# Attention by pairs of heads: scores as rounded-operand products on half the array rows, value products issued alternately into two column halves

## The reference

```python
# first network, mixers A, B and C, each with 8 heads of 64
s = einsum(q, k_all)                       # 256 latent + 256 context keys
# A: no mask;  B: + bias of the neighbourhood;  C: band mask, a sink logit per head
p = softmax(s);  y = einsum(p, v_all)
yc = einsum(softmax(einsum(qc, kc)), vc)   # context queries, first layer only
ux = concatenate([ya, yb, yc_]) * silu(px[9]);  x = x + gate * (ux @ w_out)
# second network, each layer: 8 heads over compressed, selected and window keys,
# gated and summed, and 8 heads of causal attention of its own
o = gate0 * o_cmp + gate1 * o_sel + gate2 * o_win
```

## Time and profile before

| | us |
|---|---|
| median of 3 runs | 2254.88 (2253.24 to 2255.66) |
| span of the profiled execution | 2251.3 |
| PE busy | 2108.9 (94%) |
| PE weight loads busy | 1909.6 (85%) |
| DVE busy | 1317.9 (59%) |
| ACT busy | 1136.5 (50%) |
| POOL busy | 40.8 (2%) |

### The profile page before, as it was taken

The page is one execution under the profiler, slowest core; times in us unless marked ns, Lnnn a source line. Parts: engine busy times, 40 slices in busy tenths (PEclk is TensorE's granted clock), DMA queues, the critical chain, the costliest instruction groups (busy, mean ns, idle before and its releaser), DMA issues.

```text
span 2251.3 us, 40100 instructions
## 1 busy us (share of the span) xinstructions
PE 2108.9 (94%) x15086; PEld 1909.6 (85%) x15086; DVE 1317.9 (59%) x2238; ACT 1136.5 (50%) x1994; POOL 40.8 (2%) x49
## 2 busy tenths in 40 slices
PE   6799999999799899799999999999899998989997
PEld 5767976966569776699999889999899998889997
DVE  5755238447662466566556767664665546766654
ACT  5455236256552546466354555553565445555653
POOL 2000002000000010000000000000000000000000
PEclk9899989999999999899989999999999989999999
DMA  8221223121122322155544224555455443234553
GB/s 294 110 81 60 87 93 112 64 87 57 57 75 76 126 71 75 42 183 186 182 156 150 77 94 169 178 179 185 151 180 176 173 146 114 103 121 169 186 187 131
DMA packets 41625, 289.35 MB, mean 129 GB/s; under 512 B 4656, under 2 KB 5696, under 8 KB 7440
## 3 DMA queue, kind: packets, MB, share of 16 engines
q1 hardware_dynamic: 39344, 279.99, 34.8%
q0 software_dynamic: 2144, 7.48, 1.0%
HBM read 286.40 MB, written 1.05 MB: 128 GB/s over the span
## 4 chain that ended last, share of the span: by engine, by line
PE 86%; DVE 5%; ACT 5%; issue 2%; DMA 2%; DVEq 0%; ACTq 0%; SPq 0%
PE bank L1503 23%; PE bank L1505 22%; PE bank L1504 22%; PE bank L1592 6%; PE bank L1635 5%; PE bank L1620 3%; DMA raw_panels<-weights 2%; ACT panels_hi L604 1%; DVE panels_lo L1000 1%; PE bank L1579 1%; PE bank L1571 1%; ACT kT_padded L710 1%; PE bank L1545 1%; DVE softmax_stats L1086 1%; PE bank L1555 1%
## 5 line engine op out<-in xcount | busy, mean ns | idle before, releaser
L604 ACT ACTIVATE panels_hi<-raw_panels 128x1024 fp32r<-128x1024 f32 x532 | 547.5, 1052 | 800.1 <-PE bank L1505 774.4
L1000 DVE TENSOR_TENSOR panels_lo<-raw_panels,panels_hi 128x1024 fp32r<-128x1024 f32 x532 | 641.5, 1225 | 510.1 <-ACT panels_hi L604 508.9
L1503 PE MATMUL bank<-acts_hi,panels_hi 128*128 128x256 f32 (+2 forms) x3072 | 899.1, 293 | 15.2 <-DVE acts_lo L1137 6.6
L1505 PE MATMUL bank<-acts_hi,panels_lo 128*128 128x256 f32 (+2 forms) x3072 | 891.5, 290 | 0.0
L1504 PE MATMUL bank<-acts_lo,panels_hi 128*128 128x256 f32 (+2 forms) x3072 | 891.3, 290 | 0.0
L1503 PEld LDWEIGHTS bank<-acts_hi,panels_hi 128*128 128x128 f32 x3072 | 592.2, 193 | 26.7 <-DVE xT L1273 5.5
L1504 PEld LDWEIGHTS bank<-acts_lo,panels_hi 128*128 128x128 f32 x3072 | 592.3, 193 | 8.1
L1505 PEld LDWEIGHTS bank<-acts_hi,panels_lo 128*128 128x128 f32 x3072 | 592.2, 193 | 7.5
L1503 PE MATMUL bank<-panels_hi,acts_hi 128*128 128x256 f32 (+1 forms) x1056 | 309.1, 293 | 19.3 <-DVE acts_lo L1032 19.3
L1504 PE MATMUL bank<-panels_lo,acts_hi 128*128 128x256 f32 (+1 forms) x1056 | 305.6, 289 | 0.0
L1505 PE MATMUL bank<-panels_hi,acts_lo 128*128 128x256 f32 (+1 forms) x1056 | 305.3, 289 | 0.0
(11 more groups left out here) (166 smaller groups left out, 1644.5 us busy)
## 6 DMA issues: line engine op xcount, KB each, us to landing
raw_panels<-weights SPq DMA_DIRECT2D x266, 1024.0 KB, 4.8
near_bias<-rpb POOLq DMA_DIRECT2D x16, 256.0 KB, 3.0
xT<-xin POOLq DMA_DIRECT2D x4, 512.0 KB, 5.9
out<-xT SPq DMA_DIRECT2D x1, 1024.0 KB, 4.5
consts_sb<-consts POOLq DMA_DIRECT2D x1, 789.5 KB, 8.2
small_layers<-small POOLq DMA_DIRECT2D x1, 184.0 KB, 8.1
small_sb<-small POOLq DMA_DIRECT2D x1, 168.0 KB, 8.1
smallg_sb<-smallg POOLq DMA_DIRECT2D x1, 16.0 KB, 5.4
```

The lines of the kernel that those rows point to most:

```text
L604: act.activation(slot_hi(n, a, b), raw[:, (n % 2) * PAN + a:(n % 2) * PAN + b], ACT.Copy).then_inc(hi_ready, 1)
L1000: dve.tensor_tensor(slot_lo(n, a, b), raw[:, (n % 2) * PAN + a:(n % 2) * PAN + b], slot_hi(n, a, b).bitcast(F32), ALU.subtract).then_inc(l ...
L1503: pe.matmul(dst, whi_, xhi_, start=start, stop=False, skip_group_check=True)
L1505: return pe.matmul(dst, wlo_, xhi_, start=False, stop=stop, skip_group_check=True)
```

## The change

The loop runs over **steps** instead of units. A step is one pair of heads with 128 queries (for context queries and the causal heads: one pair of heads with all 256 queries), so two units at once.

- Queries and keys are kept in two parts, rounded and low (`qT_split`, `kT_split`), without padding. A score is three products of rounded operands on the 64 rows of its head; the products of the two heads alternate.
- The value products work on 128 queries at a time for a latent pair, and the two heads, which write to the two halves of the partitions, alternate product by product.
- Four score banks instead of three; the turned probabilities of a step fill two banks and are copied by one ACT instruction over both; one output bank instead of two. The steps behind are i-2 (turnings and copy), i-3 (values), i-4 (gating, rounding), i-5 (low part).
- In the turn stage ACT makes the rounded part in one copy (`turns_hi`), DVE subtracts for the low part (`turns_lo`), and only then is the bank free. The compressed keys are split in the same way, and their scores are three products of rounded operands each.
- A woven panel is rounded and split whole in one iteration, the one after its slot. The slots are 1, 4, 7, 10 and 0, 1, 3, 4, 6, 7, 9, 10.
- A bias tile holds the two heads of a step instead of the two query blocks of a head. The zero padding of the keys, and PE's waits for it, are gone.

```diff
-    qT = sb("qT", 2048)
-    kP = sb("kT_padded", 4096)
+    qT = sb("qT_split", 2 * 2048, F32R)
+    kT = sb("kT_split", 2 * 2048, F32R)
...
+    def q_split(p, e, t0):
+        return [q_of(half, p, t0)[e] for half in range(2)]
+
+    def k_split(i, e, per, t0, t1):
+        return [kT[e * HD:(e + 1) * HD, half * 2048 + i * per + t0:half * 2048 + i * per + t1] for half in range(2)]
...
@@ attention_plan, latent steps of the first network
+            for p in range(NPAIR):
+                idx = p // 2 if gqa else p
                 for qt in range(TT):
+                    units, adds = [], []
+                    for e in range(2):
...
+                        units.append(Unit([(q_split(p, e, qt * P), k_split(idx, e, 512, 0, 512), 0, 512)],
+                                          [(0, 512, h if mixer == "C" else None, None)], masks,
+                                          [(b * P, b * P) for b in range(4)]))
+                    for b in range(4):
+                        for e in range(2):
+                            vcol = (p // 2 if gqa else 2 * p + e) * HD
+                            adds.append((e, val(b, vcol), e * 512 + b * P, P, qt * P, b == 0))
+                    steps.append(Step(units, [(0, 512)], adds, len(pairs), qt == 0, qt == 1))
...
@@ ACT, in the loop
+                j = i - 2
+                if 0 <= j < len(steps):
+                    g = g0 + j
+                    act.wait_ge(probT, now(probT, g + 1))
+                    if g >= 2:
+                        act.wait_ge(pv, now(pv, g - 1))
+                    for c, n in steps[j].copies:
+                        o = act.activation(by_head(probsT(g), c, n), by_head(prob_banks, c, n), ACT.Copy)
+                    o.then_inc(probT_out, 1)
...
@@ DVE
+        def turns_lo(b, k, hi, lo, scale=1.0):
+
+            dve.wait_ge(turn_hi, now(turn_hi, k + 1))
+            dve.scalar_tensor_tensor(lo, tile4(turn_bank(b)[:, :], lo.shape[1]), scale, hi.bitcast(F32), ALU.mult,
+                                     ALU.subtract).then_inc(turn_out, 1)
...
@@ PE, in the loop
-                    for k, (keys, c, w) in enumerate(un.keys):
-                        o = pe.matmul(score_bank(u)[:, c:c + w], un.q, keys, start=True, stop=True, skip_group_check=True)
-                    o.then_inc(scores, 1)
+                    for k in range(len(units[0].parts)):
+                        for a, b in ((0, 0), (0, 1), (1, 0)):
+                            for e in range(2):
+                                q, keys, c, w = units[e].parts[k]
+                                o = pe.matmul(score_bank(2 * g + e)[:, c:c + w], q[a], keys[b], start=a + b == 0, stop=a == 1,
+                                              skip_group_check=True)
...
+                    for k, (e, v, c, n, q0, start) in enumerate(step.adds):
+                        o = pe.matmul(out_bank[e * HD:(e + 1) * HD, q0:q0 + n], v, probsT(g)[:, c:c + n],
+                                      start=start, stop=k >= len(step.adds) - 2, skip_group_check=True)
```

More of the change, by code:

```diff
@@ L395, in program, with q_of @@
         blocks: list
-        qt: int
-        group: int
     @dataclass
-    class Group:
+    class Step:
+        units: list
+        copies: list
         adds: list
         pair: int
+        first: bool
         last: bool
         cmp: bool = False
-        head: object = None
+    def q_of(half, p, t0):
+        q = qT[:, half * 2048:(half + 1) * 2048].rearrange("p (a t) -> p a t", a=4)
+        return [q[e * HD:(e + 1) * HD, p, t0:t0 + P] for e in range(2)]
+    def q_split(p, e, t0):
+        return [q_of(half, p, t0)[e] for half in range(2)]
+    def k_split(i, e, per, t0, t1):
+        return [kT[e * HD:(e + 1) * HD, half * 2048 + i * per + t0:half * 2048 + i * per + t1] for half in range(2)]
     def attention_plan(blk, mixer, with_ctx):
-        units, groups, pairs = [], [], []
-        qv = qT[:, :].rearrange("p (a t) -> p a t", a=4)
+        steps, pairs = [], []
         def val(tt, col):
@@ L444, in attention_plan @@
-                    adds = []
+                    idx = p // 2 if gqa else p
+                    units, adds = [], []
                     for e in range(2):
                         h = 2 * p + e
-                        vcol = (h // 4 if gqa else h) * HD
-                        adds += [(e, val(2 + b, vcol), 2 * e + b, 0, b == 0) for b in range(2)]
-                    groups.append(Group(adds, len(pairs), True))
-                    pairs.append((p, 1))
-            return units, groups, pairs
@@ L459, in attention_plan @@
+                    for b in range(2):
+                        for e in range(2):
+                            vcol = (p // 2 if gqa else 2 * p + e) * HD
+                            adds.append((e, val(2 + b, vcol), e * 512 + b * T, T, 0, b == 0))
+                    steps.append(Step(units, [(0, 512)], adds, len(pairs), True, True))
+                    pairs.append((p, 1))
+            return steps, pairs
+        for p in range(NPAIR):
+            g = p // 2
             for qt in range(TT):
@@ new lines, in attention_plan @@
+                for k in range(2):
+                    for b in range(qt + 1):
+                        for e in range(2):
+                            v = VS2 + b * 256 + k * P + g * HD
+                            adds.append((e, tok[:, v:v + HD], e * 512 + (2 * k + b) * P, P, qt * P, False))
+                copies = [(k * T, P) for k in range(2)] if qt == 0 else [(0, 512)]
+                steps.append(Step(units, copies, adds, len(pairs), qt == 0, qt == 1, cmp=qt == 0))
+            pairs.append((p, 0))
@@ L487, in attention_plan @@
             pairs.append((p, 1))
-        return units, groups, pairs
-    def last_unit_of(units, g):
-        return max(i for i, u in enumerate(units) if u.group == g)
+        return steps, pairs
     def merge_gate_place(r):
@@ L655, in attention @@
         def attention(blk, mixer, with_ctx, st):
-            units, groups, pairs = attention_plan(blk, mixer, with_ctx)
-            u0, g0, p0 = st.at["units"], st.at["groups"], st.at["pairs"]
-            for i in range(len(units) + 7):
+            steps, pairs = attention_plan(blk, mixer, with_ctx)
+            g0, p0 = st.at["groups"], st.at["pairs"]
+            for i in range(len(steps) + 4):
                 for r, slot in enumerate(ADA_SLOTS if st.panels and blk == 1 else ()):
@@ L700, in attention @@
-                j = i - 6
-                if 0 <= j < len(units) and last_unit_of(units, units[j].group) == j and groups[units[j].group].last:
-                    pr = groups[units[j].group].pair
+                j = i - 2
[7 more added lines that the diff above has]
+                    o.then_inc(probT_out, 1)
@@ L1281, in _ @@
                 gate(m)
+                b = ONE["turn" + m, l].at["turns"]
+                for tt in range(nt):
+                    turns_lo(b, b, q_turned(0, tt), q_turned(1, tt), HD ** -0.5)
+                    b += 1
+                for tt in range(4 if m == "B" else 2):
+                    turns_lo(b, b, k_turned(0, m, tt), k_turned(1, m, tt))
+                    b += 1
                 attention(1, m, wctx, ONE["attn" + m, l])
@@ L1409, in _ @@
             split_panel(m0 + 3)
+            b = TWO["turn_nsa"].at["turns"]
+            for tt in range(TT):
+                turns_lo(b + tt, b + tt - 2, q_turned(0, tt), q_turned(1, tt), HD ** -0.5)
             dve.wait_ge(cm_act, now(cm_act, 2))
@@ new lines, in attention @@
+                j = i - 3
+                if 0 <= j < len(steps):
+                    g, step = g0 + j, steps[j]
+                    pe.wait_ge(probT_out, now(probT_out, g + 1))
+                    if step.first and p0 + step.pair >= 1:
+                        pe.wait_ge(omul, now(omul, p0 + step.pair))
+                    if step.cmp:
+                        pr = pairs[step.pair][0]
+                        pe.matmul(out_bank[:, 0:T], vblk[:, pr * P:(pr + 1) * P], pcT, start=True, stop=False,
```

433 lines of the change are left out of this document (199 added, 234 removed).

## The result

The changed kernel is slower, by half a per cent: 2263.6 us (median of 14 runs, 2257.8 to 2269.0) against 2253.3 for the kernel before beside it (14 runs, 2248.8 to 2256.0), ratio 1.0047, 95% interval 1.0037 to 1.0056. The forecast was 2220, faster.

The account below looks back on a forecast made before the run. PE was taken as the bound, with 86% of the chain. Attention stages -48.6, waits +5, turn stages +8.5 gave -35; 2251.3 - 35 + 3.6 = 2220 us, range 2208 to 2234, chance 0.62.

Parts of the forecast that it names:

- the second network's part of the stage times: Second network's attention: 12 us off PE per stage, 5.5 lost to tail and waits, -6.6 left, twice; stages of 86.
- Mixer B: Mixer B's stages: DVE becomes the bound at 3.65 us a step; 58.6 (-8.4) and 36.5 us (-2.8).
- POOL's 4.15 a tile: Mixer B: POOL makes a bias tile in 4.15 us, over DVE's 3.65 a step; costs 1.5 in the second layer.
- PE's step in A: Mixer A: PE's time for a two-unit step falls to 2.9 us from 4.67, and PE stays the bound.
- rival (1): Attention scores: row halves run one after the other, +0.68 us on PE's step; total 2244 us, chance 0.12.
- A and C as stages: First network's mixers A and C: A takes 53.3 and 29.7 us, C 64.9 and 38.9, by layer.
- 5 put back: Whole kernel: 5 us added back for waits in order between three engines within 10% of each other.
- Around the stages: Turn stages and the panels ahead of attention: DVE's added subtractions lengthen them, +8.5 us together.
- (2): Attention and turn stages: engines interlock less, tails of 4.5, turns +3, no 5 put back; 2200 us, chance 0.17.
- (3): Attention stages: engines wait in turn, a step takes 4.2 us even in A; total 2255 us, chance 0.04.
- (4): Mixers B and C: PE's idling drops its clock to the lower level; slower, 2303 us if lasting, chance 0.05.
- The argument against (4): PE's clock: at the lower level PE would be busy throughout, and then the clock came back in every stretch before.

Follow-up runs that it names:

- e2: Changed kernel, second network only: ACT rounds a gate panel at the front of its iteration, ahead of the copy and the exponentials; 2226.5 us.
- e4: Changed kernel, mixer B only: three bias buffers instead of two, POOL starting the next tile's load before waiting for the current one; 2265.6 us.
- e10: Changed kernel with e4's bias buffers and early loads; POOL also starts an addition only after DVE's scaling of the step three before; 2256.5 us.
- e15: e2 with both units of a step using head 0's queries and keys, so all score products share array rows 0 to 63; 2294.3 us.
- e1: Changed kernel, second network only: two output banks taken in turn by the pairs, and three score banks instead of four; 2275.6 us.

## Why the prediction was wrong

**The step that failed** is the second network's part of the stage times: "The gate panels stay. Of this 5.5 goes to a coarser tail, to the steps without a panel where DVE (4.1) passes PE (2.8), and to panels waiting for a split that now comes whole behind the exponentials. Left -6.6, twice." The order was seen and the wait named, but it was priced as a share of 5.5 us. It costs 17.5 and 15.7 us: that is what e2 takes off the two stages by moving three lines of ACT's program back to where the kernel before has them, and with them moved the stages are 87.6 for a forecast of 86. Instead of 6.6 less, each stage took 12.5 and 10.8 more. What I did not do was follow who is queued behind the rounding and the split: on DVE the panel's scaling, the gating copy, the masks and the maxima of the next step, and on PE everything that needs those. About a third of it was clock (PE's busy time fell by 6.1 and 4.3 with e2): behind PE's waits some panels ran at the lower level (products 0.21 apart from 1270.5 to 1273.1, 0.12 before and after).

**Mixer B** was mis-sized, 65.2 and 38.8 for 58.6 and 36.5, and by a mechanism that the prediction doesn't have. I charged POOL's 4.15 a tile as a delay of the tiles, 1.5 us in the second layer; e4 showed that delay to be worth nothing. What POOL costs in the second layer is that its addition stops DVE's scaling, 5.3 us by e10. The trace of the kernel before has this already, five scalings of 16; the 1.65 of the earlier trace rows is a unit whose scaling took 0.49, the unit before it took 789.73 - 787.19 = 2.54 with one of 1.36. With that gone B is 33.5 in the second layer, 3 better than forecast, and 61.5 in the first, 2.9 worse. What holds the first layer's B is open.

**What was right.** PE's step in A: forecast 2.9, measured 643.89 - 640.95 = 2.94, with scores 0.89, turnings 1.03, values 1.02 from start to start (0.88, 0.98 and 1.05 forecast, the changes of division of 0.20 and 0.1 with the first two). This is the pace of the steps at the full clock; the two before them, partly at the lower level, take 3.47 and 3.28. Scores are 512 columns side by side, so rival (1) is out; e15 shows what it would have cost, 0.69 a step at the full clock for the 0.68 given, and more than the 24 us in all. A and C as stages: 181.5 together, 186.8 forecast. The "5 put back" for waits in order had no place there.

**Around the stages** the forecast was +8.5 (its items, six times 0.8, twice 0.7 and twice 1, make 8.2) and the spans give 9.7 + 8.5 = 18.2. Between the stretches of the first network the gaps grew by 0.5 to 1.2 (C of layer 0: 485.70 - 398.40 = 87.3 before, 477.70 - 389.20 = 88.5 after), as forecast at 0.8. Ahead of A in layer 0 they grew by 4.4, of which 2.7 lie before the turn stage (the first score product starts anywhere from 145.9 to 149.5 us in the runs on record); ahead of the second network by 4.3 (1.7 forecast), behind its first attention stage by 5.5 in all. No run takes these apart, and they stay open. In all: 36.4 of the miss are the second network, 8.9 mixer B, 9.7 the rest, less 5.3 gained in A and C and the 5 put back in vain: 44.7, to 0.1 what lies between the forecast change of -35.1 in the span and the measured +9.7. With the rounding in front the kernel takes 2226.5, near the 2220 forecast, but that closeness is in part luck: A and C too long and the 5 put back offset mixer B and the work around the stages.

**The rivals.** (2), less interlock, came true in A and C alone, 5.3 below forecast. (3), no change at 2255, comes nearest to the time but not by its cause: steps did not take 4.2 in A. (4), the clock: it did fall where DVE leads, to 0.81 in B of layer 0 and 0.82 in C of layer 1, but C was no longer for that (38.3, 38.9 forecast): in the middle of it, from 859.67 us on, score and value products ran at the full clock, and the steps came every 3.8 to 4.2 us. Where PE sets the pace, in the second network, the clock took about 6 of 17.5 us and 4 of 15.7. So it came with the waits and was not their cause: e2 takes most of both away with the reorder alone. The argument against (4), that a PE which is busy throughout gets its clock back, holds less well than it was given: in e15 that took 22 us. Two sums of the rivals were off as well: half of 0.68 in 24 steps is 8 and not 12 in (1), and in (4) 2 x 2.4 + 0.5 is 5.3, which makes 38 and not 48 of 60 steps.

## What to carry to other kernels

When a loop is rewritten, look in every engine's program for work whose input is ready early (the rounding of a panel) and that now stands behind a wait for something late (the turned probabilities). The change had moved the rounding there; moving it back was worth 37 us, where the whole change had lost 10. A wait that PE shows need not be the cause; follow it back until an engine idles ahead of work that others wait for and that could be done already, and look at the order before trading one buffer for another (e1 cost 12 us). When a DVE instruction of one shape shows two durations, look at what POOL does at that moment.

## What the runs showed of the hardware

- A DVE scaling of 512 columns from SBUF to SBUF takes 0.49 us, and 1.0 to 1.44 us when it starts while a 1.27 us addition runs on POOL (mixer B of the second layer); a DVE mask with one input in PSUM keeps 0.42 beside the same addition.
- Products on the two row halves start 0.004 us apart when issued in turn and 0.010 us apart when issued three and three; the six take 0.89 and 0.92 us to the next work.
- Products that all use one row half start 0.23 us apart at the full clock (512 columns), as far apart as pairs on both halves do.
- A PE that is busy throughout can be granted the lower clock for long: 0.50 over 22.0 us with PE busy for 21.98 of them, then 1.00 over 17.8 us (e15, second layer's A). In layer 0's A of the same run 0.91 was granted.
